# A two-layer hybrid diffusion backbone step: an adaLN load ahead of the row stores, routing totals summed by PE, and token indices signalled apart from the loop counts

## What is computed

```python
x = x + gate1 * (mixed_branches @ w_out)                   # out projection
h2 = rms_norm(x, norm2_g) * (1 + scale2) + shift2          # adaLN from SiLU(cond)
x = x + gate2 * HierMoE(h2)   # top 1 of 4 groups, then top 2 of its 4 SwiGLU experts
```

## Time and profile before

| | us |
|---|---|
| median of 3 runs | 1901.49 |
| lowest and highest run | 1900.81 and 1906.64 |
| profiled execution, its own time | 1910.62 |
| its span | 1908.8 |
| DVE busy | 1198.3 (63%) |
| PE busy | 1657.5 (87%) |
| ACT busy | 893.7 (47%) |
| POOL busy | 425.7 (22%) |

### The profile page before, as it was taken

The page is one execution under the profiler, slowest core; times in us unless marked ns, Lnnn a source line. Parts: engine busy times, 40 slices in busy tenths (PEclk is TensorE's granted clock), DMA queues, the critical chain, the costliest instruction groups (busy, mean ns, idle before and its releaser), DMA issues.

```text
span 1908.8 us, 34493 instructions
## 1 busy us (share of the span) xinstructions
PE 1657.5 (87%) x13277; PEld 1112.8 (58%) x13277; DVE 1198.3 (63%) x1900; ACT 893.7 (47%) x1468; POOL 425.7 (22%) x418
## 2 busy tenths in 40 slices
PE   6799889999989974888778998899999999388776
PEld 4478766777665542434455886677776556244336
DVE  4595455777537546877665925477773584787754
ACT  3322455666541123777533226466664211377653
POOL 0033243222241201212102324322222221111102
PEclk7899999999999986999859999999999999699995
DMA  8555235532327465999624732222223553399954
GB/s 296 181 197 171 68 132 182 183 104 73 115 104 255 157 253 190 350 380 365 241 112 144 246 125 87 77 98 73 73 73 127 197 195 120 126 362 371 373 210 166
DMA packets 191106, 350.71 MB, mean 184 GB/s; under 512 B 15477, under 2 KB 98934, under 8 KB 190710
## 3 DMA queue, kind: packets, MB, share of 16 engines
q1 hardware_dynamic: 181647, 319.58, 47.8%
q0 software_dynamic: 7776, 28.32, 4.0%
q10 hardware_dynamic: 1543, 0.88, 0.2%
HBM read 287.72 MB, written 61.01 MB: 183 GB/s over the span
## 4 chain that ended last, share of the span: by engine, by line
PE 65%; DVE 12%; DMA 9%; ACT 5%; issue 5%; DVEq 2%; SPq 1%; another core or an unknown queue 1%; ACTq 0%; POOL 0%; POOLq 0%
PE PS L431 38%; PE PS L438 10%; DMA wf<-in_moe_w 5%; PE PS L1055 3%; PE PS L1039 3%; DMA arena<-in_moe_w 3%; PE PS L857 2%; PE PS L813 1%; DVE arena L2363 1%; PE PS L839 1%; PE PS L823 1%; ACT arena L1439 1%; DVE hpart L1862 1%; DVE scratch L1853 1%; DMA wf<-in_w_out 1%
## 5 line engine op out<-in xcount | busy, mean ns | idle before, releaser
L1722 POOL TENSOR_TENSOR wlo<-wf,whi 128x256 f16<-128x256 f32 (+1 forms) x268 | 278.1, 1071 | 911.4 <-ACT whi L1366 911.4
L431 PE MATMUL PS<-hpart,whi 128*128 128x320 f16 x2048 | 426.5, 301 | 15.5 <-ACT arena L1439 14.5
L431 PE MATMUL PS<-hpart,wlo 128*128 128x320 f16 x1024 | 308.0, 301 | 0.0
L431 PE MATMUL PS<-whi,hpart 128*128 128x256 f16 (+2 forms) x1568 | 298.4, 291 | 5.9 <-DVE scratch L1983 3.6
L431 PEld LDWEIGHTS PS<-hpart,whi 128*128 128x128 f16 x2048 | 191.5, 98 | 104.4 <-issue 34.9
L431 PE MATMUL PS<-wlo,hpart 128*128 128x256 f16 (+2 forms) x784 | 225.7, 290 | 0.0
L431 PEld LDWEIGHTS PS<-whi,hpart 128*128 128x128 f16 x1568 | 151.9, 98 | 65.2 <-issue 24.1
L2363 DVE TENSOR_TENSOR arena<-arena 128x2048 f16<-128x2048 f32 x66 | 149.5, 2288 | 36.0 <-ACT arena L1617 35.8
L2159 DVE TENSOR_REDUCE stat<-PS 128x1 f32<-128x640 f32 (+1 forms) x160 | 110.7, 713 | 80.3 <-PE PS L1039 77.6
L1439 ACT ACTIVATE arena<-PS,pcol 128x320 f32<-128x320 f32 x128 | 67.4, 527 | 173.3 <-PE PS L431 167.9
L1617 ACT CAST arena<-arena 128x2048 f16<-128x2048 f32 x66 | 123.4, 1897 | 41.2 <-DMA arena<-in_moe_w 28.1
(11 more groups left out here) (348 smaller groups left out, 2809.6 us busy)
## 6 DMA issues: line engine op xcount, KB each, us to landing
arena<-in_moe_w SPq DMA_DIRECT2D x66, 1024.0 KB, 9.9
arena<-in_w_ada SPq DMA_DIRECT2D x40, 1024.0 KB, 7.4
wf<-in_moe_w SPq DMA_DIRECT2D x36, 1024.0 KB, 9.8
wf<-in_w_gate SPq DMA_DIRECT2D x32, 1024.0 KB, 5.5
g_rows<-arena SPq DMA_DIRECT2D x128, 160.0 KB, 1.8
wf<-in_w_in SPq DMA_DIRECT2D x18, 1024.0 KB, 7.7
y_rows<-scratch SPq DMA_DIRECT2D x34, 512.0 KB, 8.8
arena<-g_rows SPq DMA_DIRECT2D x24, 640.0 KB, 5.1
```

The lines of the kernel that those rows point to most:

```text
L431: ins = pe.matmul(out, st, mv, start=first and n == 0, stop=last and n == 2)
L1722: ins = pool.tensor_tensor(lo[:, a:b], wf[j][:, a:b], hi[:, a:b], ALU.subtract)
```

## The change

Six edits, in both layers unless said:

- SP issues adaLN load 7 (layer 0 only) ahead of the five row stores instead of behind them.
- PE makes the running totals itself: one triangular matmul over cum and 16 more columns of zeros (cumz), and five of the matrix of ones that add tile t to all columns behind it. The sums, ranks and totals, stay in PSUM, where DVE reads them; its adds over tiles are gone.
- DVE makes all five row tiles ahead of the routing arithmetic.
- DVE signals the copied indices by a new idx_ready, behind the clipping of the chunk's experts and ahead of the pair count; route_ready now marks the pair count. PE and POOL start on idx_ready.
- The register reads move: ran_before on DVE ahead of the first residual, on PE ahead of the rank matmuls; pairs_now on PE, ACT, POOL and DVE to just ahead of each loop.
- The gate weights rcol move behind the last part_low ahead of DVE's loop.

```diff
         cum = scratch[:, 2120:2200].rearrange("p (t e) -> p t e", t=TILES)
-        acc = scratch[:, 2200:2296].rearrange("p (t e) -> p t e", t=TILES + 1)
+        cumz = scratch[:, 2120:2216]
...
-        mcol_ready, mrow_ready, total_ready, rmax_ready, hot_ready, place_ready = phases("routing_dve", 6)
+        mcol_ready, mrow_ready, total_ready, rmax_ready, hot_ready, place_ready, idx_ready = phases("routing_dve", 7)
...
                 sp.wait_ge(*xraw_ready(l, KC))
                 load(slice(1, 2), 1, 2)
+                if ahead:
+                    ada_load(l + 1, 7)
                 for tile in range(TILES):
                     sp.wait_ge(*rows_whole(l, tile + 1))
                     sp.dma_start(t["h2_rows"][P * tile:P * tile + P, :], htok[:, tile, :]).then_inc(rows_out.sem, 16)
                 if ahead:
-                    ada_load(l + 1, 7)
                     params_load(sp, l + 1)
...
+                pe.wait_ge(started.sem, 1)
+                pe.wait_ge(*base_ready(l, 1))
+                b, ran, past = ran_before(pe)
                 pe.wait_ge(*hot_ready(l, 1))
                 pe.wait_ge(*route_in(l, 16))
-                pe.matmul(bank(4)[:, 128:208], before, cum.rearrange("p t e -> p (t e)"), start=True, stop=True)
-                pe.matmul(bank(4)[:, 256:336], ones[:, :], cum.rearrange("p t e -> p (t e)"), start=True, stop=True
-                          ).then_inc(cnt_done.sem, 1)
+                pe.matmul(bank(4)[:, 128:224], before, cumz, start=True, stop=False)
+                for tile in range(TILES):
+                    n = TILES - tile
+                    ins = pe.matmul(bank(4)[:, 144 + 16 * tile:224].rearrange("p (r e) -> p r e", r=n), ones[:, :],
+                                    cum[:, tile, :].rearrange("p (o e) -> p o e", o=1).to_broadcast([P, n, EXPERTS]),
+                                    start=False, stop=tile == TILES - 1)
+                ins.then_inc(cnt_done.sem, 1)
...
                 if ahead:
                     ada_turn(l + 1, 3)
                     pe.wait_ge(*ada_done(l + 1, 1))
-
-                pe.wait_ge(started.sem, 1)
-                pe.wait_ge(*base_ready(l, 1))
-                b, ran, past = ran_before(pe)
-                pe.wait_ge(started.sem, 1)
-                pe.wait_ge(*route_ready(l, 1))
-                p = pairs_now(pe)
+                pe.wait_ge(*idx_ready(l, 1))
...
                 turn_act(0, 0, True)
+                pe.wait_ge(started.sem, 1)
+                pe.wait_ge(*route_ready(l, 1))
+                p = pairs_now(pe)
                 with pe.Fori(0, p + 1) as i:
...
-                act.wait_ge(started.sem, 1)
-                act.wait_ge(*route_ready(l, 1))
-                p = pairs_now(act)
...
                 part_high(2, 0, 1, 0)
+                act.wait_ge(started.sem, 1)
+                act.wait_ge(*route_ready(l, 1))
+                p = pairs_now(act)
                 with act.Fori(0, p + 1) as i:
...
-                pool.wait_ge(*route_ready(l, 1))
+                pool.wait_ge(*idx_ready(l, 1))
...
                 rows_from(xg[0], idxall[:, 2:3], xg_in[0])
+                pool.wait_ge(started.sem, 1)
+                pool.wait_ge(*route_ready(l, 1))
                 p = pairs_now(pool)
...
+                dve.wait_ge(started.sem, 1)
+                dve.wait_ge(*base_ready(l, 1))
+                b, ran, past = ran_before(dve)
                 dve.drain()
                 dve.tensor_copy(idw.rearrange("p a s n -> p (a s) n")[:, :, 0:P],
...
-                dve.wait_ge(started.sem, 1)
-                dve.wait_ge(*base_ready(l, 1))
-                b, ran, past = ran_before(dve)
...
+                dve.memset(cumz[:, 16 * TILES:], 0.0)
...
                 dve.tensor_tensor(cum, ohm[:, 0:5, :], ohm[:, 5:10, :], ALU.add).then_inc(hot_ready.sem, 1)
-                for tile in range(3):
+                for cs in csum:
+                    dve.memset(cs[:, 0:8], 0.0)
+                for tile in range(TILES):
                     row_tile(tile)
                 dve.wait_ge(*cnt_done(l, 1))
                 dve.wait_ge(*route_in(l, 16))
-
-                dve.memset(acc[:, 0, :], 0.0)
-                for cs in csum:
-                    dve.memset(cs[:, 0:8], 0.0)
-                dve.drain()
-                for tile in range(TILES):
-                    dve.tensor_tensor(acc[:, tile + 1, :], acc[:, tile, :], bank(4)[:, 256 + 16 * tile:272 + 16 * tile],
-                                      ALU.add)
-                    dve.drain()
-                dve.tensor_tensor(cum, bank(4)[:, 128:208].rearrange("p (t e) -> p t e", t=TILES), acc[:, 0:5, :], ALU.add)
+                ranks = bank(4)[:, 128:208].rearrange("p (t e) -> p t e", t=TILES)
+                totals = bank(4)[:, 208:224]
...
-                count(nch, acc[:, 5, :], steps[:, 1:5], ALU.is_gt, EXPERTS, 4)
+                count(nch, totals, steps[:, 1:5], ALU.is_gt, EXPERTS, 4)
...
                 ins.then_inc(place_ready.sem, 1)
-                for tile in range(3, TILES):
-                    row_tile(tile)
 
                 count(cef, iota[:, 0:CHUNKS + 1], incl, ALU.is_ge, CHUNKS + 1, EXPERTS)
                 dve.tensor_scalar(cexp[:, :], cef, float(EXPERTS - 1), None, ALU.min)
+                dve.wait_ge(*list_done(l, 1))
+                dve.tensor_copy(idxall, bank(5, CHUNKS + 2)).then_inc(idx_ready.sem, 1)
                 dve.drain()
                 dve.tensor_copy(cexp[:, 0:EXPERTS], iota[:, 0:EXPERTS])
                 count(loopf[:, 1:2], incl[:, 15:16], iota[:, 1:CHUNKS + 1:2], ALU.is_gt, 1, PAIRS + 1)
-                dve.tensor_scalar(loopi[:, 1:2], loopf[:, 1:2], -2.0, None, ALU.add)
-                dve.wait_ge(*list_done(l, 1))
-                dve.tensor_copy(idxall, bank(5, CHUNKS + 2)).then_inc(route_ready.sem, 1)
-                dve.wait_ge(*rexp_ready(l, 1))
...
-                dve.wait_ge(started.sem, 1)
-                dve.wait_ge(*route_ready(l, 1))
-                p = pairs_now(dve)
+                dve.tensor_scalar(loopi[:, 1:2], loopf[:, 1:2], -2.0, None, ALU.add).then_inc(route_ready.sem, 1)
...
                 part_low(0, 0, 6)
+                dve.wait_ge(*rexp_ready(l, 1))
+                dve.tensor_reduce(rcol[:, 3, :], ex5[:, :, 0:4], AX_X, ALU.add)
...
+                dve.wait_ge(started.sem, 1)
+                dve.wait_ge(*route_ready(l, 1))
+                p = pairs_now(dve)
                 with dve.Fori(0, p + 1) as i:
```

More of the change, by code:

```diff
@@ L2454, in _ @@
                     row16 = (None, first, iota[:, 0:EXPERTS])[by]
-                    by16 = cum if by == 0 else bc(row16.rearrange("p (o e) -> p o e", o=1), [P, TILES, EXPERTS])
+                    by16 = ranks if by == 0 else bc(row16.rearrange("p (o e) -> p o e", o=1), [P, TILES, EXPERTS])
                     dve.tensor_tensor(tb, ohm[:, 5 * ch:5 * ch + 5, :], by16, ALU.mult)
@@ L2543, in _ @@
                 part_low(0, 0, 6)
+                dve.wait_ge(*rexp_ready(l, 1))
+                dve.tensor_reduce(rcol[:, 3, :], ex5[:, :, 0:4], AX_X, ALU.add)
+                dve.tensor_scalar(rcol[:, 4, :], ex5[:, :, 4], 1.0, None, ALU.add)
+                dve.drain()
+                dve.tensor_tensor(rcol[:, 5, :], rcol[:, 3, :], rcol[:, 4, :], ALU.mult)
+                dve.drain()
+                dve.reciprocal(rcol[:, 3, :], rcol[:, 5, :])
+                dve.drain()
+                dve.tensor_tensor(rcol[:, 4, :], rcol[:, 3, :], ex5[:, :, 4], ALU.mult)
+                dve.drain()
+                for n in (3, 4):
+                    dve.tensor_scalar(rcol[:, n + 2, :], rcol[:, n, :], 1.0 / A_SCALE, None, ALU.mult)
+                dve.wait_ge(started.sem, 1)
+                dve.wait_ge(*route_ready(l, 1))
+                p = pairs_now(dve)
                 with dve.Fori(0, p + 1) as i:
```

11 lines of the change are left out of this document (removed).

## The result

| | median us | runs | ratio to the kernel before, 95% interval |
|---|---|---|---|
| before | 1901.29 (1900.81 to 1906.64) | 4 | |
| changed | 1876.57 (1873.27 to 1880.53) | 4 | 0.9865 [0.9837, 0.9892] |

The changed kernel takes 24.7 us less. The forecast was 1883.5 us and 18.0 us less; the result lies just under the low end of its range, 1877. The profiled execution took 1878.36 us, its span 1876.5.

The account below looks back on a forecast made before the run. Late adaLN load (layer 0) and DVE's routing (layer 1) bound the expert start; full DMA bounds the stage behind. Gains 17.5 + 4.3 less lap charges 1.9 + 1.9 give 18.0 us: 1901.49 to 1883.5 us, range 1877 to 1891.

Parts of the forecast that it names:

- The place that bounds: Out projection to first expert: waits on the late adaLN load (layer 0) and DVE's routing (layer 1) set the padding's start.
- A-P terms: From the end of the last x1 turn to the padding's start: 17.5 us gained in layer 0, 4.3 in layer 1.
- The gather stays under the padding: First expert's start: gather lands 4.9 us behind the index copy, padding ends 5.5 behind it, so the gather stays hidden.
- second rival: Only the first weight loads count, or gathers with loads close behind arrive late: 12.3 us gained, 1889.2 us; chance 0.13.
- First gather ends behind it: Sign of being wrong, at the first expert's start: the first gather ends later than the padding matmuls.
- What moves into the first lap: Gate weights and DVE's pair-count read, now before the first act_low, delay the weight stream: 1.9 us lost in each layer.
- first rival: Expert stage's first lap absorbs the moved DVE work at no cost: 21.8 us gained, 1879.7 us; chance 0.18.
- The sum: Whole kernel: 17.5 + 4.3 - 1.9 - 1.9 = 18.0 us gained.
- The step to a median and the range: Whole kernel: profiled 1892.6 us forecast restated from the runs' median 1901.49 as 1883.5 us, range 1877 to 1891.
- rival of 1879.7: Expert stage's first lap absorbs the moved DVE work, so 21.8 us are gained; chance 0.18.
- PE warms sooner: Layer 0 padding: PE, busy just before, reaches 2.4 GHz for its last 2.5 us; 1.2 us more, 1882.3 us; chance 0.06.

Follow-up runs that it names:

- gates_first: The changed kernel with the gate weights and DVE's read of the pair count back in front of the first cast: 1873.46 us, ratio 0.9872.
- gather_first: The changed kernel with SP's first weight loads of each expert stage held until the first gather has landed: 1877.07 us, ratio 0.9884.
- after_again: The changed kernel, unedited, run again with more rounds: 1877.27 us, ratio 0.9900 to the kernel before.

## Why the prediction was right and wrong

- **The place that bounds, right.** Both A-P terms came out: 17.6 us for 17.5, and 4.7 for 4.3, with the edits' order on each engine as foretold. Of the six edits the early load, the totals by PE and the gate weights were tried alone or undone. The early row tiles, the register reads and the separate index signal were not; their parts are argued from the timelines.
- **"The gather stays under the padding", wrong.** The step took 3.5 us for the gather; it took 8.69 in layer 0 and 4.72 in layer 1, and 3.7 and 0.5 us came back. The quickest first gather whose landing a trace gives took 4.2. Its cover of 4.1 us (5.5 less 1.4) is worked out from layer 1's times; by the prediction's own times it is 5.5 in layer 0, where the copy is at 723.8 and the padding ends at 730.7. Against gates_first, where the gather took 4.47 us, layer 0 has two causes: the weight loads close behind it (2.5 us, gather_first), and DVE's cast ahead of it (1.8 us). Late gathers behind weight loads stood in the prediction as an aside of its second rival (0.13); the cast did not. The prediction priced what the gate weights cost where they went, and nothing for what they had shielded where they stood: 1.85 us in which the gather got ahead of the first cast. "First gather ends behind it" was one of the signs it gave for being wrong.
- **"What moves into the first lap", right in its first steps, not seen in the end.** 1.9 us a layer were charged. act_low and the loads behind it did come 2.1 us later, and the seventh cast still 2 to 3 us, but by the fourteenth cast, some 50 us on, the traces show no clear difference. That favours the first rival (0.18), not by a lap that absorbs the work, but by a stage that makes up for a late start of its loads. The premise that a stage full of transfers ends later by as much as its stream starts later is thus not borne out by these traces for 2 us, and neither refuted beyond their scatter.
- **The sum, right by two errors.** From A to T 18.1 us were gained: 22.3 in A-P (0.5 more than forecast), less 4.2 in P-T that were not charged. The 3.8 charged to the laps are not in that figure and do not show behind it. That both come to 18 is luck.
- **The step to a median and the range, wrong.** This is the step that put the result outside. The low end, 1877, left 2.7 us under the rival of 1879.7, on a reference of three runs within 6 us; differences of over 5.7 us were said to be clear. The kernel before scatters over 28 us on one chip. The two later comparisons give 18.4 and 17.4 us (1895.71 to 1877.27, 1894.49 to 1877.09), the first 24.7; its ratio 0.9865 [0.9837, 0.9892] overlaps theirs. The changed kernel's median was the same in all three, within 0.7 us; what moved is the kernel before. No step of the change was found for the 6 us between. Scatter of a sample of four runs is the likely reading, and not a shown one. Another is the chip: on the other one the kernel before stood at 1902.14 (14 runs) and the three edits of the changed kernel at 1876.0 to 1877.2, which is 25 to 26 us by the medians and 20 to 23 by the ratios. On which chip the first comparison ran is not on record, so the cause of the 6 us stays open.
- **"PE warms sooner", true in part, and turned round in layer 0.** In layer 1 of the changed kernel the padding took 4.63 us (5.26 before) and in layer 0 of gates_first 4.65, granted 0.73 over its last 2.15 us; in layer 1 the wait for the gather, 1.14 us, took more than that. In layer 0 of the changed kernel the padding took 5.49 us at 0.50 as before, and the late gather let the clock fall behind it.

## What to carry to other kernels

Small work that stands between a signal and a long instruction can be what lets another engine start first. Before moving it, look at what begins in its shadow; here an indirect gather on POOL must begin ahead of DVE's two-input instruction on SBUF, and the margin was 0.08 us in one layer (0.04 in the kernel before) and missing in the other. When an edit adds work early in a stage, follow it past the first place where the distances agree again: here the third cast agreed and the seventh did not. Price a step by distances between fixed points of the trace (A-P and P-T repeated to 0.5 us here, but for one) and not by the spans, where a stage full of transfers scatters by 10 us; and take the range from that scatter.

## What was not expected of the hardware

The expert stage's speed differs between executions and layers of one kernel. The 100 us from 780 and from 1700, after_again:

```profile
780.00:880.00 100.00, 86.95 (x414) 42.25 (x412) 76.37 (x54) 70.32 (x62) 24.91 (x18) 0.95 1.01 366
```

```profile
1700.00:1800.00 100.00, 86.87 (x432) 42.70 (x431) 81.92 (x59) 75.46 (x67) 33.55 (x17) 0.99 1.04 399
```

The transfer engines are full in both, at 366 and 399 GB/s, and T-D was 193.7 and 182.3 us. In the changed kernel's first profile it was the other way round, 390 in layer 0 and 374 in layer 1, with 186.6 and 190.8. What sets the rate was not tried.
